# A six-layer transformer kernel in which VectorE's work in three mixers is put in another order

## The reference

```python
for l in range(2):                                   # first block
    h = rms_norm(x, pre_mix_norm[l]); proj = h @ w_in[l]
    # four mixers of four heads each, joined and projected by w_o:
    a = neighbourhood_attention(..., rel_bias[l])    # heads with a bias table and a column mask
    b = rms_norm(diff_attention(...), diff_subln[l]) # softmax(s1 + alibi) - lam * softmax(s2 + alibi)
    c = gqa_attention(...)                           # plain softmax, rope
    d = mla_attention(...)                           # plain softmax, latent projections
    x = x + rms_norm(concat(a, b, c, d) @ w_o[l], post_mix_norm[l])
    x = x + rms_norm(swiglu(rms_norm(x, ...)), ...)
for i in range(4):                                   # second block: swa, gla, fox, swa
    sh1, sc1, g1, sh2, sc2, g2 = split(silu(c) @ ada_w[i] + ada_b[i], 6)
    x = x + g1 * mixer(modulate(rmsnorm(x), sh1, sc1))
    x = x + g2 * swiglu(modulate(rmsnorm(x), sh2, sc2))
```

## Time and profile before

| | |
|---|---|
| median of 3 runs | 1923.15 us (1922.59 to 1923.35) |
| the profiled execution | 1922.59 us, of it the span 1920.8 us |
| TensorE busy | 1879.0 us, 98% of the span |
| VectorE busy | 1343.3 us, 70% |
| ScalarE busy | 972.8 us, 51% |
| granted TensorE clock | full speed in all 40 slices |
| the three mixers that change (us from the span's start) | layer 0: about 15 to 144; layer 1: 347 to 476; window n = 0: 680 to 772; forget gate: from 1306 |

### The profile page before, as it was taken

The page is one execution under the profiler, slowest core; times in us unless marked ns, Lnnn a source line. Parts: engine busy times, 40 slices in busy tenths (PEclk is TensorE's granted clock), DMA queues, the critical chain, the costliest instruction groups (busy, mean ns, idle before and its releaser), DMA issues.

```text
span 1920.8 us, 34589 instructions
## 1 busy us (share of the span) xinstructions
PE 1879.0 (98%) x13530; PEld 1719.4 (90%) x13530; DVE 1343.3 (70%) x2151; ACT 972.8 (51%) x1503; POOL 69.5 (4%) x82
## 2 busy tenths in 40 slices
PE   8999999999999999999999999999999999999998
PEld 7988999988999887999989799999989998979997
DVE  5758888775878867888877588886555555765555
ACT  6765334766433476533374553346554335665333
POOL 3003000000000000000000000003200000000000
PEclk9999999999999999999999999999999999999999
DMA  8538988433888832688843368875335554325552
GB/s 292 195 122 261 346 306 313 168 132 132 303 308 326 306 133 89 259 319 314 307 180 130 150 246 323 307 289 198 124 119 200 183 194 155 127 83 187 178 193 88
DMA packets 60354, 412.21 MB, mean 215 GB/s; under 512 B 8592, under 2 KB 8784, under 8 KB 11616
## 3 DMA queue, kind: packets, MB, share of 16 engines
q1 hardware_dynamic: 55728, 401.33, 56.5%
q0 software_dynamic: 4528, 9.56, 2.0%
HBM read 409.71 MB, written 3.16 MB: 215 GB/s over the span
## 4 chain that ended last, share of the span: by engine, by line
PE 84%; DVE 8%; ACT 4%; issue 2%; DVEq 2%; ACTq 1%; DMA 0%; SPq 0%
PE psu L503 34%; PE psy L666 17%; PE psy L565 6%; PE psy L557 5%; PE psy L611 4%; PE psu L520 3%; PE psm L741 3%; PE psu L726 2%; PE psy L544 2%; DVE wlo L866 2%; PE pso L712 1%; DVE x L1116 1%; PE psy L634 1%; ACT work L785 1%; ACT whi L857 1%
## 5 line engine op out<-in xcount | busy, mean ns | idle before, releaser
L857 ACT CAST whi<-raw 128x2048 fp32r<-128x2048 f32 (+1 forms) x281 | 536.3, 1908 | 620.9 <-PE psu L503 426.3
L866 DVE TENSOR_TENSOR wlo<-raw,whi 128x2048 fp32r<-128x2048 f32 (+5 forms) x296 | 645.2, 2180 | 275.7 <-ACT whi L857 274.2
L503 PE MATMUL psu<-hhi,whi 128*128 128x256 f32 x1920 | 537.0, 280 | 0.0
L503 PE MATMUL psu<-hlo,whi 128*128 128x256 f32 x1920 | 536.0, 279 | 0.0
L503 PE MATMUL psu<-hhi,wlo 128*128 128x256 f32 x1920 | 535.8, 279 | 0.0
L503 PEld LDWEIGHTS psu<-hhi,whi 128*128 128x128 f32 x1920 | 360.8, 188 | 3.0
L503 PEld LDWEIGHTS psu<-hlo,whi 128*128 128x128 f32 x1920 | 360.8, 188 | 2.4
L503 PEld LDWEIGHTS psu<-hhi,wlo 128*128 128x128 f32 x1920 | 360.8, 188 | 0.0
L1049 DVE CUSTOM_DVE_ANT_0 ada_raw<-ada_raw,cvec 128x1024 f32<-128x1024 f32 x192 | 226.8, 1218 | 2.2 <-DMA ada_raw<-ada 2.2
L666 PE MATMUL psy<-whi,ahi 128*128 128x512 f32 x528 | 210.4, 398 | 1.0 <-DVE alo L1068 0.9
L666 PE MATMUL psy<-wlo,ahi 128*128 128x512 f32 x528 | 208.1, 394 | 0.0
(11 more groups left out here) (340 smaller groups left out, 3025.6 us busy)
## 6 DMA issues: line engine op xcount, KB each, us to landing
raw<-wts SPq DMA_DIRECT2D x280, 1024.0 KB, 4.8
ada_raw<-ada SPq DMA_DIRECT2D x96, 1024.0 KB, 4.8
dense_bias<-rel_bias POOLq DMA_DIRECT2D x32, 64.0 KB, 10.1
nab<-dense_bias SPq DMA_DIRECT2D x2, 1024.0 KB, 7.7
ada_raw<-fox_rows POOLq DMA_DIRECT2D x4, 512.0 KB, 11.8
cb<-cst POOLq DMA_DIRECT2D x1, 1408.0 KB, 8.8
cb<-cst SPq DMA_DIRECT2D x1, 1056.0 KB, 9.5
x<-x_in SPq DMA_DIRECT2D x2, 512.0 KB, 4.5
```

What stands on the lines that cost most here:

```text
L503: last = mm(psu[:, bank, cc * SEQ:(cc + 1) * SEQ], a[:, cols], h[:, kt, :], start=(kt == 0 and j == 0), stop=(kt == KT - 1 and j == 2))
L857: nc.scalar.copy(whi[:, part_of(c), 0:n], raw[:, slot_of(c), 0:n]).then_inc(hi_done, 1)
L866: last = nc.vector.tensor_tensor(wlo[:, part_of(c), cols], raw[:, slot_of(c), cols], whi[:, part_of(c), cols].bitcast(f32), ALU.subtract)
```

## The change

Five edits, all of them in the order of work:

- `MIX.lo`: the low part of unit 12 moves from slot 23 to slot 22. The masks of heads 2 and 3 move from slots 24 and 25 to slot 22, behind `sub_sums` and ahead of that low part.
- `dve_steps`: the second maximum of a pair without tables is taken in the next slot, like all others, and no longer at the end of the pair's slot.
- `FOX.lead`: the order "00 10 01 11" becomes "00 01 10 11".
- `SWA`: the ada halves move from slots 18 and 22 to slots 2 and 4 (n = 0 only, since only layers up to number 3 have one here). In each slot they stand behind the low part.
- `FOX`: the low part of unit 2 moves from ahead of the mixer to behind the move of the logits out of PSUM.

```diff
--- before.py
+++ after.py
@@ -80,16 +80,15 @@
 
 MIX = Plan([2 if u is None else 4 for u in W_IN1], [3, 3, 2] + [2] * 11 + [1] * 20 + [2] * 4, range(12, 32),
            [24, 25, 28, 29, 30, 31, 33, 35], "00 01 10 02 03 11 12 13",
-           [2, 3, 5, 7, 10, 11, 13, 14, 18, 23, 26, 30, 34], 24)
+           [2, 3, 5, 7, 10, 11, 13, 14, 18, 22, 26, 30, 34], 24)
 FOX = Plan([4] * 13, [3, 4, 1] + [2] * 30, [9, 10, 11, 12, 13, 14, 15, 16, 17, 18, 19, 20, 23, 24, 25, 26],
-           [14, 16, 18, 20, 26, 27, 28, 30], "00 10 01 11 02 12 03 13", None, 23)
+           [14, 16, 18, 20, 26, 27, 28, 30], "00 01 10 11 02 12 03 13", None, 23)
 SWA = Plan([4] * 6, [2] * 8 + [1] * 15 + [2, 2, 1, 2, 2], range(6, 22), [11, 13, 15, 17, 20, 21, 23, 25],
            "00 01 10 02 03 11 12 13", [2, 4, 6, 8, 13, 17, 20, 24], 16)
 GLA = Plan([4] * 13, [3, 4, 1] + [1] * 60, [], [45, 46, 49, 50, 52, 53, 55, 57], "00 10 01 11 02 12 03 13",
            [2, 3, 7, 11, 16] + list(range(19, 63, 4)))
 GLA_LEVEL = {16: 0, 18: 1, 22: 2, 26: 3, 30: 4, 34: 5, 38: 6}
 GLA_STATE = {39: 1, 40: 2, 41: 3}
-NEIGHBOUR_MASKS = {19: 0, 21: 1, 24: 2, 25: 3}
 SWA_ROPE = {1: 0, 3: 1, 7: 2, 11: 3, 15: 4}
 SWA_HEADS = {3: 0, 5: 1, 9: 2, 13: 3, 17: 4}
 
@@ -825,19 +824,13 @@
 
         def dve_steps(dve, I0, items, plan, h, g):
             k = plan.score(h)
-            second = None
             if k is not None:
-                pair = plan.joint[k] and items[k]["table"] is None
-                if not pair or k % 2 == 0:
-                    if items[k]["tpre"] is not None:
-                        dve.wait_ge(*items[k]["tpre"])
-                    dve_negated(dve, I0, items[k], k, score_at(plan, k))
-                    second = k + 1 if pair else None
+                if items[k]["tpre"] is not None:
+                    dve.wait_ge(*items[k]["tpre"])
+                dve_negated(dve, I0, items[k], k, score_at(plan, k))
             k = plan.value(h)
             if k is not None:
                 dve_divide(dve, I0, items[k], k)
-            if second is not None:
-                dve_negated(dve, I0, items[second], second, score_at(plan, second))
             if h in plan.turn:
                 dve_turn(dve, plan.turn[h], g)
 
@@ -1423,11 +1416,12 @@
                 nc.vector.tensor_tensor(dh4, dh4, gain64.unsqueeze(1).unsqueeze(1).to_broadcast([P, NT, 4, HD]),
                                         ALU.mult).then_inc(mix_ready, 1)
 
-            def neighbour_mask(head):
+            def neighbour_mask(h0, n):
                 dve.wait_ge(na_loaded, 16 * (l + 1))
-                bias = fold(nab[:], NT, 4, 4, 64)[:, :, head]
-                mask = cb[:, CB1["na"][0]:CB1["na"][1]].unsqueeze(1).unsqueeze(1).to_broadcast([P, NT, 4, 64])
-                nc.vector.tensor_tensor(bias, bias, mask, ALU.add)
+                for h in range(h0, h0 + n):
+                    bias = fold(nab[:], NT, 4, 4, 64)[:, :, h]
+                    mask = cb[:, CB1["na"][0]:CB1["na"][1]].unsqueeze(1).unsqueeze(1).to_broadcast([P, NT, 4, 64])
+                    nc.vector.tensor_tensor(bias, bias, mask, ALU.add)
 
             for h in range(MIX.slots):
                 dve_steps(dve, I0, items, MIX, h, l)
@@ -1445,12 +1439,15 @@
                     head_rope()
                 if h == 15:
                     latent_rope()
+                if h == 19:
+                    neighbour_mask(0, 1)
+                if h == 21:
+                    neighbour_mask(1, 1)
                 if h == 22:
                     sub_sums()
+                    neighbour_mask(2, 2)
                 if h == 23:
                     sub_norm()
-                if h in NEIGHBOUR_MASKS:
-                    neighbour_mask(NEIGHBOUR_MASKS[h])
                 if h in MIX.lo:
                     dve_lo(dve, l, MIX.lo[h] + SPLIT)
                 if h in (16, 20):
@@ -1840,8 +1837,8 @@
                          fold(s_u, NT, 256), fold(s_v, NT, 256), 32).then_inc(swa_rope, 1)
                 if h in SWA.lo:
                     dve_lo(dve, DEPTH1, c0 + SWA.lo[h] + SPLIT)
-                if h in (18, 22) and g < ADA_LAYERS:
-                    dve_ada(dve, g, 0, (h - 18) // 4)
+                if h in (2, 4) and g < ADA_LAYERS:
+                    dve_ada(dve, g, 0, h // 2 - 1)
 
         def dve_fox(dve, n, c0, b0):
             I0, g = item0[n], DEPTH1 + n
@@ -1852,6 +1849,7 @@
                     dve.wait_ge(unit_mm, unit_no(DEPTH1, c0) + 1)
                     nc.vector.tensor_scalar(f_x, psy[0:16, 0, 0:SEQ], pcol2[0:16, 16 * DEPTH2:16 * DEPTH2 + 1], None,
                                             ALU.add).then_inc(bank_free, 1)
+                    dve_lo(dve, DEPTH1, c0 + 2)
                     dve.wait_ge(fox_l, 1)
                     nc.vector.scalar_tensor_tensor(out=f_lf, in0=f_x, scalar=0.0, in1=f_l, op0=ALU.min, op1=ALU.subtract)
                     nc.vector.drain()
@@ -2091,7 +2089,8 @@
                     dve_columns(dve, 0, 0)
                     dve_root_scales(dve, 2 * g, DEPTH1, 1)
                 dve_split(dve, 2 * g)
-                dve_lo(dve, DEPTH1, c0 + 2)
+                if kind != "fox":
+                    dve_lo(dve, DEPTH1, c0 + 2)
                 dve.wait_ge(cb2_loaded, 16)
                 {"swa": dve_swa, "gla": dve_gla, "fox": dve_fox}[kind](dve, n, c0, b0)
                 for which, end, ahead in ((0, c0 + nin + 3, c0 + nin + 5), (1, c0 + nin + 4 + FFN_UNITS - 1, c0 + nin + 4 + FFN_UNITS + 1)):
```

## The result

The changed kernel takes **1938.78 us** (median of five runs, 1938.29 to 1943.36), the kernel before 1922.71 beside it (1922.59 to 1923.35). The ratio is 1.0087, with a 95% interval of 1.0076 to 1.0098: slower by 16.1 us. The forecast was 1933.0 with a range to 1936.0. The side was right, the size was not: the loss is 1.6 times the 9.77 us of the sum, and the time lies outside the range.

What follows compares the result with a forecast made beforehand. TensorE, busy 98% of the span, was taken as the bound. Waits of 5.98 + 1.41 + 2.38 = 9.77 us on the profiled 1922.59 gave 1932.4, and 0.56 for the median gave 1933.0 us, range 1929.0 to 1936.0.

Steps and rivals of the forecast that it cites:

- the sum: Whole kernel: losses of 5.98 (first mixer, two layers), 1.41 (window mixer) and 2.38 (forget-gate mixer), 9.77 us together.
- TensorE is the bound, and waits add up: Whole kernel: TensorE busy 98% of the span, 41.8 us uncovered; edits on other engines lose whatever they make it wait.
- First mixer, 2.99 in each layer: Slot 22: second maximum behind masks and lo half, so score pair 12 starts at 100.99 instead of 98.00, 2.99 us late.
- neither half does it alone: First mixer: reordered maximum alone costs nothing; masks and lo half alone delay divide and norm about 2 us.
- relief: Rival: work leaving slots 24, 25 (2 x 1.20) and 18, 22 (4.8) wins 7.2 us, 1916.0; chance 0.02.
- Window mixer, 1.41: Window mixer, n = 0: second ada half delays the first maximum and a score 1.56 us; 0.15 given back, net 1.41.
- Forget-gate mixer, 2.38: Forget-gate mixer: new quarter order costs 0.78 us; with the lo half behind the gate's evacuation, 2.38 in all.
- rival (1): First mixer: waits of some 3.2 us before pair 12 make TensorE's clock fall, 1936.0 us; chance 0.08.
- 2 x 1.49: First mixer, both layers: cost of a cold array, from fourteen zero matmuls taking 4.68 us at the start, 3.19 later.
- half of the idle length of the start: Argument against a clock fall: the wait before pair 12 lasts some 3.2 us, the start's idle time 6.72.
- Hidden maximum: Rival, first mixer: second maximum costs nothing because ScalarE or TensorE come later; only 1.41 + 2.38 remain, 1927.0; chance 0.07.

Runs made afterwards that it cites:

- e2_moves: Kernel before with only the two masks and the low part of unit 12 moved to slot 22: 1926.77 us, ratio 1.0019.
- e3_second: Kernel before with only the second maximum of a pair taken in the next slot: 1924.15 us, ratio 1.0003.
- e4_mixer: Kernel before with both first-mixer edits (masks and low part moved, second maximum in the next slot), nothing else: 1935.24 us, ratio 1.0066.
- e1_fill: Changed kernel with zero matmuls in TensorE's long waits, thirteen per first-mixer layer, six in the window mixer: 1933.14 us, ratio 1.0053.
- e5_ada: Kernel before with only the window mixer's ada halves moved from slots 18 and 22 to 2 and 4: 1925.99 us, ratio 1.0012.
- e8_best: Kernel before with first-mixer sums of squares ahead of the second maximum and a window-mixer lo half moved from slot 8 to 9: 1920.98 us, ratio 0.9988.

## Why the prediction was wrong, step by step

- **TensorE is the bound, and waits add up.** Right. Its waits cost 9.33 us in the profile; the sum was 9.77. With the idle time filled, 9.5 are left in the profile and 10.0 by the medians.
- **First mixer, 2.99 in each layer.** Right to 0.07, and by the chain that was worked out: masks, lo half, second maximum, exponential, pair 12. That neither half does it alone was right too (e2_moves, e3_second, e4_mixer). In e2_moves the lateness at the first turn is 1.4 and 1.2 us and not 2. The relief that the edit brings in slots 24 and 25 gives nothing back.
- **Window mixer, 1.41.** The wait is split, as was allowed for, 0.63 ahead of the transposes and 0.82 more at the third score pair, and the pair is 1.63 late (1.56 forecast). Net it is 1.12 against 1.41: the prediction gave back only 0.15, since behind the pair it had all in step, and passed over the wait of 0.94 at 724.31, which shrinks by 0.39.
- **Forget-gate mixer, 2.38.** Measured 2.31: 0.70 for the order (0.78 forecast) and 1.61 for the lo half (1.60).
- **The clock: this step failed.** The sum has no term for matmuls that run slower behind a wait. That was rival (1), put at "2 x 1.49" behind the two pairs 12, and given 0.08. The runs showed 5.9 us in its place (table; 5.6 to 6.0 by e1_fill), at three places. Two things were wrong. First the weight: "half of the idle length of the start" was set against it, but 6.72 us was only the one idle length that the profile of before offers. It shows slow matmuls after 6.72, and nothing of what happens after 3.25. The full granted clock in all slices of before spoke neither way: behind the start its longest wait is 1.19, and at the start itself the view is blind. By stretches of the kernel before:

```profile
8.00:10.00 2.00, 2.00 (x7) 0.78 (x6) 0.83 (x3) 1.34 (x2) 0.00 (x0) 1.00 1.05 430
10.00:12.00 2.00, 2.00 (x14) 1.38 (x13) 0.84 (x1) 0.00 (x0) 0.00 (x0) 1.00 1.02 430
```

Both rows say 1.00, but the zero matmuls start 0.43 us apart up to 9.69 and 0.22 apart from 9.94 on: they ran at half speed first. So the slow level could be seen in this trace, by the spacing of equal matmuls. Second the size: 1.49 was taken from fourteen zero matmuls at the start, as if a fall always cost the same. It cost 1.58, 2.78 and 1.53, somewhat less than half of the time at the lower level (3.4, 6.8 and 3.4 us), and it reached a place with a wait of 1.89 that the rival left out. With the clock in the forecast as rival (1) had it, 1936.0, the result would still have been 2.8 us above it.
- The rule of the Trainium skill that was weighed there ("TensorE: Matmul & The Clock Gate", Part 1: The HAM clock gate), that an idle array drops to half its clock and earns it back by work, agrees with the trace: 0.50 behind the wait of 3.25, and full speed again while TensorE works (0.80 in the stretch 444 to 446, in which it is busy throughout). That outcome came, and the argument against it was the weaker one.
- **Hidden maximum, relief.** Both fell: pair 12 waits for the exponential in both layers, and of the 7.2 us of relief almost nothing came back (0.12 at the wait of 0.15).

Left open is what decides in the single case. Behind the same wait of 1.96 the clock fell in one layer and not in the other, and behind the same waits of 1.19 and 0.40 in one profile of twelve. The runs show the odds (3.25: each time, in both layers of two kernels' profiles; 1.89 to 1.96: five of six; 1.07 to 1.44 alone: never in these profiles), not the rule. Nor do they show why one fall lasts 3.4 us and another 6.8. The slowest execution of the changed kernel, 1943.36, has a mean granted clock of 0.993 where the other four of the five have 0.995 or 0.996, so more falls in it are likely, but it was not profiled.

## What to carry to other kernels

Where TensorE bounds the kernel, a wait of it costs its own length and, from about 2 us on, mostly another 1.5 to 3.1 us of slow matmuls behind it; price a new wait of that size with both, and look at the granted clock in stretches of 2 us, since 40 slices hide it. Where such a wait can't be removed, zero matmuls in it win the second part back (5.6 to 6.0 us here for 32 of them). Two moves on VectorE that cost little one by one (2.6 and 0.6 us here, by their profiles) can be costly together (10.3), when both put work ahead of the same instruction: write down what stands ahead of each instruction for which TensorE waits, and take the sum for the whole change.

## What the runs showed of the hardware

- The clock can fall behind the end of a wait. In e5_ada the wait of 1.91 us ends at 716.54, and the stretch from 716 to 718 is still at full clock; the slow one is 718 to 722. The matmuls right behind a wait can look healthy. It can also fall within the wait: in layer 1 of the changed kernel the stretch 438 to 440 is at 0.50 throughout, and the wait ends at 438.61.
- A fall can follow waits far shorter than the first suspect: in e8_best, 1.19 and 0.40 us with eight matmuls between them, for 1.6 us of loss. It did not in eleven other profiles with the same waits.
- Fourteen zero matmuls at the start took from 4.53 to 6.12 us in thirteen profiles, which alone moves the time of an execution by up to 1.6 us. The granted clock of the view reads 1.00 there in the kernel before, while equal matmuls start first 0.43 and then 0.22 us apart.
